# A two-block network on one core: roots applied behind the projections, x in chunks, transposes between pieces

## The chip, the cores and the metric

The kernel runs on one core of a Trainium2 chip, in one launch. The metric is the time of the launch on the device in microseconds. Three runs of the kernel before gave 2681.14, 2683.04 and 2679.93 us, median 2681.14.

## The reference, cut to what matters

Two small networks of two layers each are applied to one sequence of 256 tokens and 2048 features, in float32. The change touches the first network alone:

```python
def first_block(x, ...):                   # x: (1, 256, 2048)
    for layer in range(2):
        h = rmsnorm(x, norm_gains[layer])  # x * rsqrt(mean(x^2) + eps) * gain
        x = x + (even_layer if layer == 0 else odd_layer)(h, ...)
    return rmsnorm(x, final_norm_gain)
```

The even layer projects h to a recurrent branch (x part and gate, a convolution over 4 tokens, two gate matrices, a scan) and to sliding-window attention (q, k, v, gate), and projects the mix back. The odd layer projects h to latents with norms of their own (from which the queries, keys and values of one attention come), to a gate for it, and to a differential attention (q, k, v, gate), and projects back. Since a projection is linear, the root of a token can be multiplied before it (into h) or behind it (into its result).

## The kernel before

**Stages and pieces.** The list `STAGES` (line 52) holds the projections in order: lru, kv, swa, out0 (layer 0), cq, diff, mla, out1 (layer 1), then ret, four, out2, conv, out3 (second network). A stage has units (4 in lru, swa, out0, diff and mla, 3 in cq, 1 in kv), and a unit has 8 pieces, or 16 in diff. A piece is a weight tile of mostly 128x1024 floats (512 KB). All pieces go through a ring of four slots: SP loads `w_raw`, ScalarE rounds it to `w_hi` (line 712), VectorE computes `w_lo` = `w_raw` - `w_hi` (line 1334), and TensorE multiplies w_hi by the high part of the activations, w_hi by the low part, and w_lo by the high part (lines 2010 to 2013 where features are the rows of the result, 2025 to 2028 where tokens are). ScalarE may write a slot when the piece four before is used, SP may load it when w_lo of that piece is done.

**Order.** Each engine walks the pieces in the order of the stages and runs a hook behind each piece p of a unit. In it the epilogue of the unit before is done, step by step (functions `lru`, `swa`, `cq`, `diff`, `mla`, one of each name per engine): the eviction of the projections from PSUM in the hook of piece 2, scores on TensorE in the hook of piece 0 (swa) or 1 (diff, mla), the largest scores, exponentials, transposes and values later. In the last unit of a stage the epilogue lies in the hooks of the next stage; in mla two steps of diff share one hook. The order is written out by hand, and each engine executes strictly in its order. Most pieces let TensorE begin with w_hi alone; the last piece of a unit, and the first in stages with more than two banks (diff among them; mla is exempt), wait for w_lo first (`project`, lines 2057 to 2059).

**Banks.** lru, swa, cq and the out stages have two pairs of banks, used in turn (`PAIRS`, line 64); kv, diff and mla have one set. `enter` (line 2031) is TensorE's wait for the eviction of a bank's contents, counted by `s_free`. In diff the banks are 0 (q), 1 (k), 2 and 3 (v and gate of each tile of 128 tokens); in mla bank 2 takes the gate in pieces 0 to 3, and the others are filled later.

**The ada sums.** For the second network VectorE multiplies 256 KB pieces of a weight by two condition vectors, two operations of 128x512 a step (line 1323). `_units` (line 79) says behind which pieces: in swa 0, 1, 5, 6; in out0 from unit 1 and in cq from unit 1 all; in diff 0 to 4 and 9 to 13; in mla 4 to 7 from unit 1. The step stands behind the hook of its piece.

**The entries of both layers.** `norm` on TensorE (line 2228) transposes x, 32 blocks of 128x128, into the banks 0 to 6 (pairs of features tiles), broadcasts the roots of the tokens with a matmul of ones by a diagonal matrix (line 2251), and transposes the last pair. ScalarE has squared x (line 725 for the first layer; line 755 chunk by chunk for the others), VectorE computes the root with one Newton step (`root`), then multiplies each transposed tile by gain and root (line 1389), ScalarE rounds it (line 718), VectorE takes the difference (line 1399). SP first loads the two tiles of x, then weights; ScalarE's queue loads 15 sets of parameter rows, and GpSimd's queue constants, sinks, decays, lambdas and the gate weights.

Of the kernel before, what the change touches and what calls it, by code (L numbers as in the profile page):

```python
# [28 lines left out]
N_PARAM, N_MISC = (7, 8), 7  # L29
# [34 lines left out]
PAIRS = {"lru": ((0, 1), (2, 3)), "swa": ((2, 3), (0, 1)), "cq": ((0, 1), (2, 3)), "four": ((2, 3), (0, 1)),  # L64
# [98 lines left out]
def build(nc, d, out, stop_after=None):  # L163

    ctx = ExitStack()
    with ctx:
# [43 lines left out]
        acc_c = sb("acc_c", [P, 2, ADA_N])  # L210
        cn = sb("c_norm", [P, CQ_T + CKV_T, 2 * T], F32R)
# [63 lines left out]
        s_par = [sem("first_params_landed"), sem("other_params_landed")]  # L275
        s_ident = sem("identity_landed")
        s_misc = sem("small_inputs_landed")
        s_x = [sem(f"x_landed{t}") for t in range(TT)]
# [25 lines left out]
        s_n = {k: sem(f"norm_{k}") for k in ("sum", "mean", "root", "diag", "rows", "rows_sb", "psum", "tile", "hi", "lo")}  # L304
        s_added = sem("residual_added")
# [9 lines left out]
        for stage, names in {  # L315
            "lru": ("conv", "gates", "gate", "tanh", "sig", "y"),
            "swa": ("gate", "scores", "max", "exp", "prob", "probT", "probT_sb", "o", "y"),
# [48 lines left out]
        NORM_BANKS = {0: 0, 1: 8, 3: 16, 4: 24, 5: 32}  # L366

# [52 lines left out]
        def _(sp):  # L420
            for t in range(TT):
                sp.dma_start(x[:, t, :], d["x"][0, t * P:(t + 1) * P, :]).then_inc(s_x[t], 16)
# [4 lines left out]
            def sources(stage, i, p):  # L427
# [29 lines left out]
                if stage == "cq":  # L457
                    w = d["l1_w_in"].rearrange("(t p) n -> p t n", p=P)
                    n = 320 if isinstance(i, int) and i == 2 else 512
                    return [(lambda r: r[:, 0:2 * n].rearrange("p (t n) -> p t n", t=2),  # L460
                             w[:, 2 * p:2 * p + 2, ds(512 * i, n)])]
# [72 lines left out]
        def view(ap, *dims):  # L534
            names = " ".join("abc"[:len(dims)])
            return ap.rearrange(f"p ({names}) -> p {names}", **dict(zip("abc", dims)))

# [108 lines left out]
        def _(pool):  # L646
            nc.gpsimd.memset(y[:, 0:3 * P], 0.0)
            nc.gpsimd.memset(ones[:, :], 1.0).then_inc(s_set, 1)
            pool.dma_start(const_a[:, :], d["const_a"][:, P:]).then_inc(s_misc, 16)
# [12 lines left out]
            gates(0)  # L662
            with pool.Fori(1, COUNT["lru"]) as i:
# [38 lines left out]
        def _(sc):  # L702
# [17 lines left out]
            def norm_sums(k, src, ready):  # L720

                for t in range(TT):
                    ready(t)
                    nc.scalar.drain()
                    last = nc.scalar.activation(scr_a[:, 0:D] if k == 0 else junk, src[:, t, :], ACT.Square,
                                                accum_out=stat[:, 0, t:t + 1])
                last.then_inc(s_n["sum"], 1)
# [10 lines left out]
            def norm_hi(k, dst, order, bias=None):  # L738

                buffers = norm_scratch(k)[0]  # L740
                for n in order:
                    tmp = halves(buffers[:, n % buffers.shape[1], :])
                    sc.wait_ge(s_n["tile"], NORM_BANKS[k] + n + 1)
                    if bias is None:
                        last = copy(dst[:, 2 * n:2 * n + 2, 0:T], tmp)
                    else:
                        for h in range(2):
                            last = nc.scalar.activation(dst[:, 2 * n + h, 0:T], tmp[:, h, :], ACT.Identity,
                                                        bias=bias(2 * n + h))
# [539 lines left out]
        def _(ve):  # L1289
# [213 lines left out]
            def kv(p, i=0):  # L1503
                pass
# [1103 lines left out]
```

## Time and profile before

| | |
|---|---|
| median of three runs | 2681.14 us (2679.93 to 2683.04) |
| span of the profiled execution | 2678.8 us (first to last instruction) |
| TensorE matmuls | 2612.4 us, 98% |
| VectorE | 1708.0 us, 64% |
| ScalarE | 1280.1 us, 48% |
| GpSimd | 23.0 us, 1% |
| DMA | 536.51 MB, 200 GB/s in the mean |

The profile gives the span of one execution; its whole time lies in what the runs show, 1.1 to 4.2 us above the span. The page gives for each engine its busy time; for the matmuls the ends are modelled, so that overlapping ones are counted once. In the list of waits of an engine each row is a line that waited, the line it waited for, the total in us, how often and the longest. In a timeline a row is start and duration in us, engine, line, operation, result <- operands and the number of merged instructions; a bracket shows the idle time of the engine before it and what released it.

### The profile page before, as it was taken

What the parts mean: (1) busy time and instruction counts of PE and PEld (TensorE: products, weight loads), DVE (VectorE), ACT (ScalarE), POOL (GpSimd) and SP (SyncE); (2) the same over time, 40 slices, a digit from 0 to 9 for tenths busy, and PEclk for the clock granted to TensorE, in tenths of its full rate; (3) what the DMA queues carried; (4) which work ended last, traced back from release to release, by engine and by line L of the source; (5) the groups of instructions that cost most, each with busy time, mean ns of one, the idle gap of its engine ahead of it and who ended that gap; (6) DMA issues with size and microseconds to landing.
All of it is one profiled execution on the core that took longest, in us unless ns stands there. A gap on an engine that the chain in (4) does not pass through costs nothing.

```text
span 2678.8 us, 40094 instructions
## 1 busy us (share of the span) xinstructions
PE 2612.4 (98%) x14747; PEld 2292.4 (86%) x14747; DVE 1708.0 (64%) x2212; ACT 1280.1 (48%) x1795; POOL 23.0 (1%) x42
## 2 busy tenths in 40 slices
PE   7999999999999999999999999999999999999998
PEld 6999878888977899999999988878888888888886
DVE  5768888875786755455556565567875555555644
ACT  4767444555557444344453344444444444444443
POOL 1000000000000000000000000000000000000000
PEclk9999999999999999999999999999999999999999
DMA  6565867874666555555566766657975556566664
GB/s 190 163 208 174 271 196 235 249 233 134 208 222 200 178 179 187 166 180 178 179 196 224 230 199 204 191 173 258 295 255 185 187 188 189 188 190 188 207 192 141
DMA packets 451671, 536.51 MB, mean 200 GB/s; under 512 B 33147, under 2 KB 343958, under 8 KB 450646
## 3 DMA queue, kind: packets, MB, share of 16 engines
q1 hardware_dynamic: 448128, 522.29, 62.0%
q0 software_dynamic: 2720, 12.21, 1.5%
q8 instruction: 85, 1.39, 0.2%
q10 hardware_dynamic: 694, 0.26, 0.0%
q14 instruction: 44, 0.36, 0.0%
HBM read 532.56 MB, written 2.10 MB: 200 GB/s over the span
## 4 chain that ended last, share of the span: by engine, by line
PE 91%; DVE 4%; ACT 2%; issue 1%; DMA 1%; DVEq 1%; ACTq 0%; SPq 0%
PE banks L2025 20%; PE banks L2026 20%; PE banks L2028 20%; PE banks L2010 7%; PE banks L2013 7%; PE banks L2011 7%; DVE w_lo L1334 1%; PE banks L2454 1%; DMA w_raw<-in_l_w_in 1%; PE banks L2212 1%; ACT w_hi L712 1%; PE banks L2509 1%; PE banks L2495 1%; PE banks L2485 1%; PE banks L2475 1%
## 5 line engine op out<-in xcount | busy, mean ns | idle before, releaser
L1334 DVE TENSOR_TENSOR w_lo<-w_raw,w_hi 128x1024 fp32r<-128x1024 f32 (+2 forms) x840 | 975.1, 1168 | 653.1 <-ACT w_hi L712 623.6
L712 ACT ACTIVATE w_hi<-w_raw 128x1024 fp32r<-128x1024 f32 (+2 forms) x840 | 842.9, 1013 | 903.8 <-PE banks L2028 744.4
L2025 PE MATMUL banks<-w_hi,act_hl 128*128 128x512 f32 (+2 forms) x2496 | 961.8, 386 | 8.8 <-DVE scr_a L1389 2.5
L2026 PE MATMUL banks<-w_hi,act_hl 128*128 128x512 f32 (+2 forms) x2496 | 956.5, 384 | 0.0
L2028 PE MATMUL banks<-w_lo,act_hl 128*128 128x512 f32 (+2 forms) x2496 | 693.4, 383 | 0.0
L2025 PEld LDWEIGHTS banks<-w_hi,act_hl 128*128 128x128 f32 x2496 | 471.0, 189 | 99.2 <-issue 3.7
L2026 PEld LDWEIGHTS banks<-w_hi,act_hl 128*128 128x128 f32 x2496 | 471.4, 189 | 83.9 <-issue 0.2
L2028 PEld LDWEIGHTS banks<-w_lo,act_hl 128*128 128x128 f32 x2496 | 457.5, 189 | 83.4
L2010 PE MATMUL banks<-act_hl,w_hi 128*128 128x256 f32 x1696 | 446.8, 293 | 15.1 <-ACT scr_a L718 4.9
L2011 PE MATMUL banks<-act_hl,w_hi 128*128 128x256 f32 x1696 | 431.0, 284 | 0.0
L2010 PEld LDWEIGHTS banks<-act_hl,w_hi 128*128 128x128 f32 x1696 | 325.5, 192 | 28.0 <-issue 14.2
L2011 PEld LDWEIGHTS banks<-act_hl,w_hi 128*128 128x128 f32 x1696 | 326.1, 192 | 4.0 <-issue 0.7
L2013 PE MATMUL banks<-act_hl,w_lo 128*128 128x256 f32 x1696 | 288.6, 285 | 0.0
L2013 PEld LDWEIGHTS banks<-act_hl,w_lo 128*128 128x128 f32 x1696 | 251.1, 192 | 4.8
L718 ACT ACTIVATE scr_b<-banks 128x512 f32<-128x512 f32 (+1 forms) x112 | 56.3, 504 | 93.2 <-PE banks L2478 34.8
L1323 DVE SCALAR_TENSOR_TENSOR acc_x<-y_mix,silu_c,acc_x 128x512 f32<-128x512 f32 x120 | 89.6, 746 | 1.7
L1323 DVE SCALAR_TENSOR_TENSOR acc_x<-const_b,silu_c,acc_x 128x512 f32<-128x512 f32 x120 | 89.5, 746 | 1.5
L1323 DVE SCALAR_TENSOR_TENSOR acc_c<-ada_ring,silu_c,acc_c 128x512 f32<-128x512 f32 x120 | 89.5, 746 | 0.6
L1323 DVE SCALAR_TENSOR_TENSOR acc_x<-ada_ring,silu_c,acc_x 128x512 f32<-128x512 f32 x120 | 89.4, 745 | 0.0
L718 ACT ACTIVATE scr_a<-banks 128x512 f32<-128x512 f32 (+3 forms) x64 | 38.4, 640 | 44.0 <-PE banks L2311 30.6
L850 ACT ACTIVATE scr_a<-scr_a,soft 128x128 f32<-128x128 f32 x80 | 35.3, 442 | 29.1 <-DVE soft L1522 29.1
L1005 ACT ACTIVATE scr_b<-banks 128x256 f32<-128x256 f32 x16 | 6.0, 382 | 78.5 <-PE banks L2454 78.5
(301 smaller groups left out, 1589.7 us busy)
## 6 DMA issues: line engine op xcount, KB each, us to landing
w_raw<-in_od_w_in SPq DMA_DIRECT2D x256, 512.0 KB, 4.0
w_raw<-in_ev_w_in SPq DMA_DIRECT2D x256, 256.0 KB, 3.6
w_raw<-in_l_w_in SPq DMA_DIRECT2D x96, 512.0 KB, 4.4
w_raw<-in_l_w_in SPq DMA_DIRECT2D x128, 256.0 KB, 3.5
ada_ring<-in_ada_w SPq DMA_DIRECT2D x128, 256.0 KB, 4.2
w_raw<-in_l_w_out SPq DMA_DIRECT2D x64, 512.0 KB, 4.7
y_mix<-in_ada_w SPq DMA_DIRECT2D x128, 256.0 KB, 3.1
const_b<-in_ada_w SPq DMA_DIRECT2D x128, 256.0 KB, 4.7
```

The costliest lines, as they stand in the source:

```text
L712: last = nc.scalar.activation(dst(w_hi[:, p % RING, :]), src(w_raw[:, p % RING, :]), ACT.Copy)
L718: return nc.scalar.activation(dst, src, ACT.Copy, **k)
L850: last = nc.scalar.activation(v[:, h, lo:hi], v[:, h, lo:hi], ACT.Exp, bias=soft[:, 1, 2 * h + b:2 * h + b + 1], accum_out=soft[:, 2, 2 * ...
L1323: last = stt(acc, w, cond, acc, ALU.mult, ALU.add)
L1334: last = tt(dst(w_lo[:, p % RING, :]), src(w_raw[:, p % RING, :]), dst(w_hi[:, p % RING, :]).bitcast(F32), ALU.subtract)
L2010: mm(out, hi, a[:, kt, 0:T], start=start, stop=False, skip_group_check=True)
L2011: r = mm(out, hi, a[:, kt, T:2 * T], start=False, stop=False, skip_group_check=True)
L2013: r = mm(out, lo, a[:, kt, 0:T], start=False, stop=stop, skip_group_check=True)
L2025: mm(out, ah, hi, start=start, stop=False, skip_group_check=True)
L2026: r = mm(out, al, hi, start=False, stop=False, skip_group_check=True)
L2028: r = mm(out, ah, lo, start=False, stop=stop, skip_group_check=True)
L2212: last = mm(PS[:, bank, at:at + 1], acc[:, b * P:(b + 1) * P], ones[:, 0:1], start=True, stop=True, skip_group_check=True)
```

## The change

1. SP loads x in four chunks of 512 features (both token tiles), each ahead of one of the first weight pieces, and takes over most parameter rows, behind pieces 3, 4 and 5. ScalarE's queue loads the identity and the gains alone. GpSimd waits for two used pieces before its loads, and loads the constants last.
2. In the first network x is transposed without the root: ScalarE rounds gain times x from PSUM, VectorE computes the difference from PSUM. The pairs of tiles are transposed between the pieces of the first unit of lru, and, for the second layer, between pieces of the last unit of out0 and the first of cq, in another order of the features (`TURN_ORDER`), with the weights of cq in that order.
3. The root is computed meanwhile and broadcast to `root_row`. Where the result has tokens in the free dimension (lru, kv's keys, q and gate of swa, q and k of diff, gate of mla), VectorE evicts it, times `root_row` (`leave`, `mla_gate`); where tokens are the partitions (values of kv, cq, v and gate of diff), ScalarE evicts it with the root as scale.
4. cq's pairs of banks are exchanged, and TensorE's waits are fitted.

```diff
-PAIRS = {..., "cq": ((0, 1), (2, 3)), ...
+PAIRS = {..., "cq": ((2, 3), (0, 1)), ...
 def _(sp):
-            for t in range(TT):
-                sp.dma_start(x[:, t, :], d["x"][0, t * P:(t + 1) * P, :]).then_inc(s_x[t], 16)
+            x_chunk(0)
...
                         for dst, src in pieces:
                             sp.dma_start(dst(w_raw[:, p % RING, :]), src).then_inc(s_w[p % RING], 16)
+                        if stage == "lru" and first == 0 and p < 3:
+                            x_chunk(p + 1)
+                        if stage == "lru" and first == 0 and 3 <= p < 6:
+                            parameter_rows(p - 3)
...
 def _(pool):
-            pool.dma_start(const_a[:, :], d["const_a"][:, P:]).then_inc(s_misc, 16)
+            pool.wait_ge(s_used, 2)
...
             gates(0)
+            pool.dma_start(const_a[:, :], d["const_a"][:, P:]).then_inc(s_misc, 16)
...
 def _(sc):
+            def turned_high(k, n):
+                pair, b = TURN_ORDER[k][n], turned_bank(k, n)
+                sc.wait_ge(s_n["psum"], NORM_BANKS[k] + n + 1)
...
+                for h in range(2):
+                    last = copy(act[:, 2 * pair + h, 0:T], half_of(b, h), scale=pcol(gains, 2 * pair + h))
+                last.then_inc(s_n["hi"], 1)
 def lru
-                if p == 2:
+                if p == 3:
                     sc.wait_ge(s["y"], i + 1)
-                    full(sc, "lru", i, 1)
-                    copy(lru_x[:, :, 3:259], halves(pair_bank("lru", i, 0))).then_inc(s_free, 1)
-                    full(sc, "lru", i, 2)
-                    copy(lru_g, pair_bank("lru", i, 1)).then_inc(s_free, 1)
+                    sc.wait_ge(s_free, bank_count("lru", i, 2))
 def diff
                     sc.wait_ge(s["y"], i + 1)
-                    full(sc, "diff", i, 1)
-                    copy(at_q, bank(A), scale=64 ** -0.5).then_inc(s_free, 1)
-                    full(sc, "diff", i, 2)
-                    copy(at_k, bank(B)).then_inc(s_free, 1)
+                    sc.wait_ge(s_free, bank_count("diff", i, 2))
                     full(sc, "diff", i, 3)
-                    copy(at_v[:, 0:T], half_of(C, 0))
+                    copy(at_v[:, 0:T], half_of(C, 0), scale=stat[:, 3, 0:1])
...
+            split("lru")(0, placed({
+                0: highs(0, 0, 1), 1: highs(0, 2), 2: highs(0, 3), 3: highs(0, 4),
+                4: [*highs(0, 5), lambda: input_square(0)],
+                5: [*highs(0, 6), lambda: input_square(1).then_inc(s_n["sum"], 1)],
+                6: [*highs(0, 7), lambda: norm_root(0)]}))
...
 def _(ve):
+            def turned_low(k, n):
+                ve.wait_ge(s_n["hi"], NORM_BANKS[k] + n + 1)
+                for h in range(2):
+                    f = 2 * pair + h
+                    last = stt(act[:, f, T:2 * T], half_of(b, h), pcol(gains, f), act[:, f, 0:T].bitcast(F32),
+                               ALU.mult, ALU.subtract)
...
+            def leave(stage, i, n, dst, scale=None):
+                full(ve, stage, i, n)
+                src = halves(pair_bank(stage, i, n - 1) if stage in PAIRS else bank(BANKS[stage][n - 1]))
+                if scale is None:
+                    r = tt(dst, src, root_by_token(), ALU.mult)
+                else:
+                    r = stt(dst, src, scale, root_by_token(), ALU.mult, ALU.mult)
+                r.then_inc(s_free, 1)
 def lru
                 if p == 2:
-                    ve.wait_ge(s_free, bank_count("lru", i, 1))
+                    drain()
+                    leave("lru", i, 1, lru_x[:, :, 3:259])
+                    leave("lru", i, 2, halves(lru_g))
+                    drain()
 def swa
+                if p == 2:
+                    drain()
+                    leave("swa", i, 1, halves(swa_q), SWA_D ** -0.5)
+                    leave("swa", i, 2, halves(swa_g))
 def diff
+                if p == 2:
+                    drain()
+                    leave("diff", i, 1, halves(at_q), 64 ** -0.5)
+                    leave("diff", i, 2, halves(at_k))
...
+            def mla_gate(i):          # called in the hook of piece 7 of unit i
+                drain()
+                ve.wait_ge(s_used, pieces_before("mla", i) + 4)
+                tt(halves(at_g), halves(bank(C)), root_by_token(), ALU.mult).then_inc(s_free, 1)
...
+            split("lru")(0, placed({
+                0: lows_of(0, 0, 1), 1: lows_of(0, 2), 2: lows_of(0, 3), 3: lows_of(0, 4), 4: lows_of(0, 5),
+                5: lows_of(0, 6), 6: [*lows_of(0, 7), lambda: block_root(0)],
+                7: [first_parameters, lambda_sums, clear_history]}))
...
 def _(te):
+                if stage == "diff" and isinstance(i, int) and i == 0:
+                    v = bank_count("cq", 1, 2) if n < 3 else bank_count("cq", 2, n - 2)
...
+            gain_columns()
+            turn(0, 0)
+            turn(0, 1)
+            stage_loop(te, "lru", run("lru"), lru_and_columns, placed({
+                **{p: turns(0, p + 2) for p in range(5)}, 5: [*turns(0, 7), first_columns], 6: [lambda: root_rows(0)]}))
...
+                def turns_in_out0(p, i):
+                    if i == COUNT["out0"] - 2 and 1 <= p < 7:
+                        turn(1, p - 1)
...
-                norm(1, x, first_columns, lambda: te.wait_ge(s_free, BANK0["cq"]))
-                run("cq")(0, nothing, 0)
+                run("cq")(0, placed({1: turns(1, 6), 2: turns(1, 7), 6: [lambda: root_rows(1)]}), 0)
```

## Rows read from the trace of the kernel before

**Rows 1.** The page, part 1: busy time, share and instructions of each engine.
```profile
PE 2612.4 (98%) x14747; PEld 2292.4 (86%) x14747; DVE 1708.0 (64%) x2212; ACT 1280.1 (48%) x1795; POOL 23.0 (1%) x42
```
**Rows 2.** Waits of TensorE over the span: total us, times, longest.
```profile
PE banks L2010 <- ACT scr_a L718: 4.9, 4, 2.1
...
PE banks L2025 <- ACT scr_a L928: 0.8, 2, 0.4
```
**Rows 3.** Timeline of the start and of the second unit of lru.
```profile
18.27 1.06 ACT L712 ACTIVATE w_hi<-w_raw 128x1024 fp32r<-128x1024 f32 x1 [2.73 <-DMA w_raw<-in_l_w_in]
22.82 0.58 PE L2010 MATMUL banks<-act_hl,w_hi 128*128 128x256 f32 x1 [3.63 <-DVE act_hl L1399]
48.24 0.55 PE L2010 MATMUL banks<-act_hl,w_hi 128*128 128x256 f32 x1 [2.85 <-DVE w_lo L1334]
54.81 1.12 PE L2013 MATMUL banks<-act_hl,w_lo 128*128 128x256 f32 x8
57.69 1.12 PE L2013 MATMUL banks<-act_hl,w_lo 128*128 128x256 f32 x8
```
**Rows 4.** Line 422, the two loads of x: from issue to landing.
```profile
DMA to landing us min/median/max: 5.2/7.2/9.2
```
**Rows 5.** Timeline: a square of x, two tile products, an output product.
```profile
10.00 1.91 ACT L725 ACTIVATE scr_a<-x_res 128x2048 f32<-128x2048 f32 x1
24.94 0.87 DVE L1389 SCALAR_TENSOR_TENSOR scr_a<-banks,param_cols,scr_a 128x256 f32<-128x256 f32 x2
199.24 0.69 DVE L1555 TENSOR_TENSOR y_mix<-banks,scr_a 128x512 f32<-128x512 f32 x1 [3.82 <-PE banks L2319]
```
**Rows 6.** Stretches: length, busy times (count), granted clock, DMA share, GB/s.
```profile
22.82:27.82 5.00, 5.00 (x23) 5.00 (x24) 3.77 (x6) 2.52 (x3) 0.00 (x0) 0.51 0.47 150
48.24:52.68 4.44, 4.43 (x24) 4.44 (x25) 3.37 (x3) 3.53 (x5) 0.00 (x0) 0.62 0.61 174
629.00:640.00 11.00, 8.89 (x63) 8.32 (x63) 4.83 (x5) 5.22 (x7) 0.00 (x0) 0.84 0.52 172
420.00:430.00 10.00, 8.29 (x58) 7.93 (x57) 9.63 (x15) 5.86 (x12) 0.00 (x0) 1.00 0.97 317
```
**Rows 7.** Timeline of out0 to cq and of cq to diff.
```profile
344.96 1.22 DVE L1334 TENSOR_TENSOR w_lo<-w_raw,w_hi 128x1024 fp32r<-128x1024 f32 x1
354.85 3.22 PE L2238 MATMUL banks<-ident,x_res 128*128 128x128 f32 x28
364.08 0.80 PE L2025 MATMUL banks<-w_hi,act_hl 128*128 128x512 f32 x1 [2.49 <-DVE scr_a L1389]
427.78 0.36 PE L2010 MATMUL banks<-act_hl,w_hi 128*128 128x256 f32 x1 [1.71 <-DVE w_lo L1334]
```
**Rows 8.** Timeline in unit 2 of swa: scores, and w_lo of pieces 2, 3.
```profile
205.07 1.68 PE L2304 MATMUL banks<-scr_a 64*128 64x128 f32 x16
206.26 2.36 DVE L1334 TENSOR_TENSOR w_lo<-w_raw,w_hi 128x1024 fp32r<-128x1024 f32 x2
```
**Rows 9.** Timeline where units 1 and 2 of diff begin.
```profile
475.74 1.23 DVE L1334 TENSOR_TENSOR w_lo<-w_raw,w_hi 128x1024 fp32r<-128x1024 f32 x1
477.43 0.50 PE L2025 MATMUL banks<-w_hi,act_hl 128*128 128x512 f32 x1
527.21 0.28 PE L2010 MATMUL banks<-act_hl,w_hi 128*128 128x256 f32 x1
528.72 1.23 DVE L1334 TENSOR_TENSOR w_lo<-w_raw,w_hi 128x1024 fp32r<-128x1024 f32 x1
527.49 1.28 ACT L928 ACT_TABLE_LOAD   x1
528.78 0.39 ACT L928 ACTIVATE scr_a<-banks 128x256 f32<-128x256 f32 x1
529.22 0.50 PE L2025 MATMUL banks<-w_hi,act_hl 128*128 128x512 f32 x1 [0.41 <-ACT scr_a L928]
```
**Rows 10.** Timeline at the end of mla: scores of the last unit.
```profile
762.23 1.66 PE L2411 MATMUL banks<-k_rope,scr_a 64*128 64x128 f32 x8 [4.58 <-DVE scr_a L1636]
```

More of the change, by code:

```diff
@@ L718, in copy, with input_square @@
                 return nc.scalar.activation(dst, src, ACT.Copy, **k)
[L720 to L727, printed above, removed]
+            def input_square(t):
+                if t == 0:
+                    for c in range(4):
+                        sc.wait_ge(s_x[c], 16)
+                nc.scalar.drain()
+                return nc.scalar.activation(scr_a[:, 0:D], x[:, t, :], ACT.Square, accum_out=stat[:, 0, t:t + 1])
+            def turned_high(k, n):
+                pair, b = TURN_ORDER[k][n], turned_bank(k, n)
+                gains = G_L0 if k == 0 else G_L1
+                sc.wait_ge(s_n["psum"], NORM_BANKS[k] + n + 1)
+                if k == 0 and n == 0:
+                    sc.wait_ge(s_pc, 1)
+                if k == 1:
+                    sc.wait_ge(s_used, pieces_before("out0", 3) + pair + 1 if pair >= 4 else pieces_before("out0", 0))
+                for h in range(2):
+                    last = copy(act[:, 2 * pair + h, 0:T], half_of(b, h), scale=pcol(gains, 2 * pair + h))
+                last.then_inc(s_n["hi"], 1)
             def root_table():
@@ L742, in norm_hi @@
                     tmp = halves(buffers[:, n % buffers.shape[1], :])
[L743 to L749, printed above, removed]
+                    sc.wait_ge(s_n["tile"], NORM_TILES[k] + n + 1)
+                    for h in range(2):
+                        last = nc.scalar.activation(dst[:, 2 * n + h, 0:T], tmp[:, h, :], ACT.Identity,
+                                                    bias=bias(2 * n + h))
                     last.then_inc(s_n["hi"], 1)
@@ L959, in mla @@
                     full(sc, "mla", i, 5)
-                    copy(at_g, bank(C)).then_inc(s_free, 1)
+                    sc.wait_ge(s_free, bank_count("mla", i, 1))
                     copy(mla_qr0, PS[:, 4, 0:T], scale=MLA_SCALE).then_inc(s_free, 1)
@@ L1503, in kv @@
             def kv(p, i=0):
-                pass
+                if p == 2:
+                    full(ve, "kv", 0, 2)
+                    for g in range(2):
+                        last = tt(kT4[:, 2 * g:2 * g + 2, :], halves(bank(A))[:, g:g + 1, :].broadcast_to([P, 2, T]),
+                                  root_by_token(), ALU.mult)
+                    last.then_inc(s_free, 1)
             def scores_max(s_tile, heads, mask, first_bank, done, sink=None):
@@ L2253, in norm, with turn @@
                 r.then_inc(s_n["rows"], 1)
[L2254 to L2255 removed]
+            def turn(k, n):
+                pair, b = TURN_ORDER[k][n], turned_bank(k, n)
+                if k == 0:
+                    te.wait_ge(s_x[n // 2], 16)
+                else:
+                    te.wait_ge(s_free, bank_count("out0", 3 - pair // 2, 2))
+                buffers = 4 if k == 0 else 3
+                if n >= buffers:
+                    te.wait_ge(s_n["lo"], NORM_BANKS[k] + n - buffers + 1)
+                for h in range(2):
+                    f = 2 * pair + h
+                    for t in range(TT):
+                        c = h * T + t * P
+                        r = nc.tensor.transpose(PS[:, b, c:c + P], x[:, t, f * P:(f + 1) * P], ident[:, :])
+                r.then_inc(s_n["psum"], 1)
             def context_pair(b):
```

244 lines of the change are left out of this document (138 added, 106 removed).

## Prediction

> **What bounds the kernel now.** I read the page first: TensorE is busy for 2612.4 of the 2678.8 us [rows 1], so only what stops TensorE, or slows its clock, can be gained or lost. The waits of TensorE come next [rows 2]: evictions that hold it up are there already (4.9 us before line 2010, 0.8 us before line 2025). Then the timelines. At the start TensorE stands until 22.82, and again for 2.85 us before 48.24 [rows 3]. Between pieces it repeats one pattern: the low products start at 54.81 and again at 57.69, so a piece costs 2.88 us at full clock [rows 3]. Everything else that counts is how far VectorE and ScalarE are ahead of TensorE where one unit follows another, since both walk the pieces in order and do a unit's epilogue in the hook of the next unit's piece 2.
>
> The clock. In the stretch behind a 3.63 us stop it is granted at 0.51, behind 2.85 us at 0.62, behind 2.11 us at 0.84 over 11 us, and behind 1.71 us (420 to 430) at 1.00 [rows 6]; 0.5 is 1.2 GHz, 1.00 is 2.4 GHz. So a stop of over 2 us costs (1 - 0.51) x 5.0 = 2.5, (1 - 0.62) x 4.44 = 1.7 or (1 - 0.84) x 11 = 1.8 us more, and one of 1.7 us nothing. I take 1.8 for a long stop and half of it for one of 1.9 to 2.0 us, which lies between. The Trainium skill (TensorE: Matmul & The Clock Gate, Part 1) says that the place where the clock changes shifts from run to run; by that the half stops could come out either way in different runs.
>
> **Part 1, the start (a gain).** The first piece waited for all of x (2 MB, landing after 5.2 and 9.2 us, 7.2 in the middle [rows 4]), its sums, the root, and for the weights, which landed only at 18.27 behind x and everything else [rows 3]. Now 512 KB of x and then piece 0 stand first in SP's queue, the parameter rows follow piece 3, and GpSimd's broadcasts and constants wait for two used pieces. Half of a tile that took 5.2 us should be there at 4 to 5 us, the weights at 6 to 7: I take 6.4. Then w_hi 1.06 [rows 3], w_lo 1.23 [rows 9], two lows 0.87 [rows 5], each behind the other on VectorE: 6.4 + 3.2 = 9.6 for the first product, against 22.82; bounds 8.5 and 12. From there to the end of the ninth piece: 9 x 2.88 = 25.9; a cold first piece 2.2 (as before, part of the 2.5); 24 transposes at 3.22/28 = 0.115 us [rows 7], 2.8; the row sums of the roots and a parameter transpose 0.6. Then the stops that stay: ScalarE's two squares of 1.91 us and a read each [rows 5] stand ahead of w_hi of pieces 5 and 6 (about 0.5 each), and the root chain on VectorE stands ahead of w_lo of piece 7, which the last piece of a unit wants whole (2.4). Sum 9.6 + 25.9 + 2.2 + 2.8 + 0.6 + 3.4 = 44.5; before it was 54.81 + 0.96 = 55.8 [rows 3]. Gain 11.3. Behind it the parameter arithmetic on VectorE (some 4 us), two evictions more and the copied root row no longer lie under that slack: I give back 1.8 in units 1 and 2, and 0.8 for half a clock fall at piece 7. Net gain 8.7 (bounds 5 and 12).
>
> **Part 2, out0 to cq (a gain).** Before, out0's last product ends where the first of 28 transposes starts, at 354.85; the root and the rest follow, and cq starts at 364.08 [rows 7], with a piece of 12 products at the low clock (2.5 us by rows 6). Now latent transposes stand between pieces, with the scales applied behind. 364.08 - 354.85 = 9.2, plus 2.5, less 32 transposes (3.7) and the root rows (0.5): 7.5. VectorE does two lows more (1.7 us) in out0's last unit, in which it is otherwise full; it had w_lo of the last piece done at 346.2 [rows 7] and TensorE took it at 352.1, so they are covered. Bounds 5 and 8.5.
>
> **Part 3, cq to diff (a gain).** The 1.71 us before 427.78 [rows 7] end with ScalarE's eviction of cq's last unit: diff's first bank was the same one. With the bank pairs of cq exchanged, diff's banks 0 and 1 are free: 1.7. Bounds 0.5 (VectorE carries the root copy in cq) and 1.7.
>
> **Part 4, mla's gate (a small gain).** The gate's bank is full after piece 3 and was copied only after piece 7. Copied by VectorE in the same unit's piece 7, it is free before the next unit: of the four waits of 4.9 us in [rows 2] the longest, 2.1, is diff to mla, and the other three, 2.8 together, go. Behind the last unit TensorE waits 4.58 us for VectorE's rope [rows 10], and the copy (0.69 [rows 5]) stands ahead of that: -0.75. Net gain 2.0.
>
> **Part 5, the evictions moved to VectorE (a loss).** The root must be multiplied along the free dimension, so q and k of diff, q and gate of swa and both of lru now leave PSUM on VectorE, in the hook of piece 2, that is behind w_lo of piece 2. ScalarE was ahead there; VectorE isn't, since it has two steps of the ada sums (2 x 0.75 us each) between w_lo of pieces 0, 1 and 2. One leave is a tensor-tensor of 128x512 out of PSUM, 0.69 us [rows 5].
>
> swa: scores stand behind piece 0 of the next unit and want q. In unit 2 they started at 205.07, while w_lo of pieces 2 and 3 ran from 206.26 (2.36 for both) [rows 8]: piece 2 is done at 207.48, q leaves at 208.2, so TensorE stops 3.15 us and loses 1.8 of clock: 4.9. The pattern repeats twice, less late: in unit 3 without a mix in between (scores at 233.11, w_lo from 233.16, q out at 235.1: 2.0) and in out0, where scores come at once (258.28; w_lo of piece 2 ends at 259.43, q out at 260.15: 1.9). Both 1.9 to 2.0: another 2 x 0.9. Sum 10.6. The first unit is free of it (VectorE has no output to wait for).
>
> diff: one set of banks, so piece 0 of the next unit itself wants bank 0. In unit 2 TensorE was there at 527.21 [rows 9]; w_lo of piece 2 starts at 528.72 and ends at 529.95, q is out at 530.7, k at 531.3: a stop of 3.5 us. Now ScalarE, which waits for k, does v (as long as the silu), loads a table (1.28) and does the first silu (0.39) [rows 9] before bank 2 is free: 533.4, while it was entered at 529.22. That is 4.2 us, and 0.4 for what is left of the low clock. Unit 3 repeats it (w_lo of piece 2 from 578.75): 4.7. At unit 1 VectorE is less late (w_lo of piece 2 from 475.74 [rows 9], TensorE ready at 475.81): bank 0 at 477.7, bank 2 at 480.45 against 477.43 [rows 9], so 3.0 + 0.3. At diff to mla ScalarE's chain moves by 0.4. Sum 13.0. Bounds: nothing, if something keeps VectorE ahead that I don't see; 16, with each clock fall full.
>
> lru: two leaves more (1.4 us) before the convolution, whose result is wanted only behind piece 2, where it had over 3 us: free. VectorE's kT4 and ScalarE's scaled v4 in kv: free, for swa's first banks are others.
>
> For one step a page speaks against what I took: the Trainium skill (ScalarE: Activation LUTs, What ACT_TABLE_LOAD costs) puts a table switch at 1.28 us and 1.38 us of drain. The row shows the silu 0.01 us behind the load [rows 9]: no drain. By the page each of four joins would be 1.4 us worse, 5.5 us in all; nothing here rests on it.
>
> **Sum.** -8.7 - 7.5 - 1.7 - 2.0 + 10.6 + 13.0 = +3.7 us. The profile's span is 2678.8 and the runs, with what lies around it, 2679.93 to 2683.04, median 2681.14, so 2.3 us around; the forecast is 2678.8 + 3.7 + 2.3 = 2684.8. The change moves some 20 us out of two joins and the start and puts 24 us into six others.
>
> **The rivals.** (a) Faster: VectorE's lateness costs half or less. It would take stops that overlap with others or a VectorE that comes earlier to piece 2; for it speaks that its ada steps wait for nothing, so any slack comes back to it. The place is the hook of piece 2 in swa and diff, and it decides when part 5 is below 14 us: at half, 2681.1 + 3.7 - 11.8 = 2673. With part 5 at nothing it is 2661. Against it: before each of these joins VectorE waits for something that answers to TensorE (the output of the unit before, or ScalarE's w_hi that waits for a used piece), so its distance to TensorE is fixed. (b) Clearly slower: the start brings little. VectorE waits in piece 7 of the first unit for seven small inputs, among them 0.7 MB of constants, which GpSimd now issues at 19 us or later; TensorE wants w_lo of the next piece at about 44. If they land after 42, or the first weights at 9 us, the start gives 4 instead of 8.7, and every clock fall comes full: 2684.8 + 4.7 + 3 = 2692. (c) The join of out0 and cq turns into a new stop, since ScalarE waits there for transposes before w_hi of the next pieces: 2 to 4 us, 2688.
>
> **Chances.** The forecast (gains and stalls as summed, within 3 us) 0.55; (a) 0.17; (b) 0.13; (c) 0.15. No change within 0.2% means 2675.8 to 2686.5, which is about what a measurement of this kernel can tell. Of the forecast's 0.55 about 0.4 lies in it, of (a) 0.03, of (c) 0.04; faster 0.14 from (a); the rest, 0.39, is slower. Range for 8 in 10: 2673 to 2692, from (a) at half cost to (b).
>
> **What would show it.** The first product at 9 to 10 us, the ninth piece done near 45. No stop between out0 and cq. New stops of TensorE before the scores of swa (3.1, 2.0, 1.9 us) whose releaser is VectorE's new eviction line, and before piece 0 of diff's units 1 to 3 (2, 3.5, 3.5 us), each followed by a wait for ScalarE's silu. The prediction is wrong if those stops are below 1 us, if the first product comes after 12 us, or if mla's three waits stay.

## The result, and the profile after

The changed kernel took 2687.61 us (median of 9 runs, 2685.54 to 2690.48) against 2681.14 us of the kernel before (9 runs, 2678.03 to 2684.06). The ratio is 1.0027, with a 95% interval of 1.0019 to 1.0036: slower, by a little more than can be told from no change. The forecast was 2684.8 us. The profiled execution took 2687.05 us over a span of 2685.4, so 1.65 us lie around the span, where the prediction had taken 2.3.

The page says only that TensorE is still nearly always busy [rows 1]; its busy time is 3.9 us longer, for nearly the same number of products (below, the same 16 products take 3.09 us at the low clock and 1.69 at the full one):

```profile
PE 2616.3 (97%) x14748; PEld 2294.3 (85%) x14748; DVE 1716.8 (64%) x2227; ACT 1270.1 (47%) x1783; POOL 23.1 (1%) x42
```

The waits of TensorE (total, times, longest) name what is new. L1471 is VectorE's new eviction `leave` with a scale; L1719 is the rope, L764 a copy of ScalarE:

```profile
PE banks L2103 <- DVE scr_a L1471: 8.9, 3, 3.5
PE banks L2415 <- DVE scr_a L1471: 7.5, 3, 3.5
PE banks L2523 <- DVE scr_a L1719: 5.7, 1, 5.7
...
PE banks L2103 <- ACT scr_a L764: 3.0, 1, 3.0
PE banks L2103 <- DVE act_hl L1448: 2.3, 1, 2.3
```

16.4 us of waits end with the eviction, for the scores of three units of swa (the last of them lies in out0) and for three units of diff. In the timeline of the start, the first product is at 10.11 where it was at 22.82 [rows 3], behind w_hi, w_lo and two low conversions, one behind the other; the last row is the later stop for w_lo of piece 7:

```profile
5.87 1.97 PE L2367 MATMUL banks<-ident,x_res 128*128 128x128 f32 x8
6.96 1.06 ACT L758 ACTIVATE w_hi<-w_raw 128x1024 fp32r<-128x1024 f32 x1 [3.62 <-DMA w_raw<-in_l_w_in]
8.05 1.22 DVE L1372 TENSOR_TENSOR w_lo<-w_raw,w_hi 128x1024 fp32r<-128x1024 f32 x1 [1.88 <-ACT w_hi L758]
9.19 1.65 DVE L1448 SCALAR_TENSOR_TENSOR act_hl<-banks,param_cols,act_hl 128x256 fp32r<-128x256 f32 x4
10.11 0.58 PE L2103 MATMUL banks<-act_hl,w_hi 128*128 128x256 f32 x1 [2.28 <-DVE act_hl L1448]
38.37 0.36 PE L2103 MATMUL banks<-act_hl,w_hi 128*128 128x256 f32 x1 [0.51 <-DVE w_lo L1372]
```

Where out0 becomes cq, the transposes lie between pieces and no bracket with idle time stands anywhere near; before there was a block from 354.85 to 364.08 [rows 7]:

```profile
357.22 0.60 PE L2367 MATMUL banks<-ident,x_res 128*128 128x128 f32 x4
357.58 0.48 PE L2118 MATMUL banks<-w_hi,act_hl 128*128 128x512 f32 x1
360.43 0.39 PE L2118 MATMUL banks<-w_hi,act_hl 128*128 128x512 f32 x1
```

The joins in swa (timeline, unit 2, and the stops of the other two). VectorE finishes w_lo of piece 2 at 198.4, has a gap of 0.45 us for which the profile names no cause, and evicts q until 199.55; TensorE stands for 3.54 us in all, and the 16 score products take 3.09 us where they took 1.68 [rows 8], at the low clock:

```profile
197.19 1.23 DVE L1372 TENSOR_TENSOR w_lo<-w_raw,w_hi 128x1024 fp32r<-128x1024 f32 x1
198.86 0.69 DVE L1471 SCALAR_TENSOR_TENSOR scr_a<-banks,root_row 128x512 f32<-128x512 f32 x1 [0.45 <-issue]
199.61 3.09 PE L2415 MATMUL banks<-scr_a 64*128 64x128 f32 x16 [3.54 <-DVE scr_a L1471]
232.25 3.01 PE L2415 MATMUL banks<-scr_a 64*128 64x128 f32 x16 [2.05 <-DVE scr_a L1471]
260.98 1.69 PE L2415 MATMUL banks<-scr_a 64*128 64x128 f32 x16 [1.92 <-DVE scr_a L1471]
```

In diff, unit 2. VectorE ends an ada step, does w_lo, then the two evictions; ScalarE waits 5.64 us for the second and only then copies v, loads a table and does the silu, for which TensorE stops again:

```profile
525.52 0.75 DVE L1361 SCALAR_TENSOR_TENSOR acc_x<-ada_ring,silu_c,acc_x 128x512 f32<-128x512 f32 x1
526.36 1.23 DVE L1372 TENSOR_TENSOR w_lo<-w_raw,w_hi 128x1024 fp32r<-128x1024 f32 x1
527.69 0.69 DVE L1471 SCALAR_TENSOR_TENSOR scr_a<-banks,root_row 128x512 f32<-128x512 f32 x1
528.29 0.68 DVE L1469 TENSOR_TENSOR scr_a<-banks,root_row 128x512 f32<-128x512 f32 x1
528.52 0.36 PE L2103 MATMUL banks<-act_hl,w_hi 128*128 128x256 f32 x1 [3.51 <-DVE scr_a L1471]
529.06 0.47 ACT L764 ACTIVATE scr_a<-banks,stat 128x256 f32<-128x256 f32 x1 [5.64 <-DVE scr_a L1469]
529.54 1.28 ACT L972 ACT_TABLE_LOAD   x1
530.83 0.47 ACT L972 ACTIVATE scr_a<-banks,stat 128x256 f32<-128x256 f32 x1
531.36 0.80 PE L2118 MATMUL banks<-w_hi,act_hl 128*128 128x512 f32 x1 [0.59 <-ACT scr_a L972]
```

The other two joins stop 1.92 us and then 1.17 us (472.20, 475.03), and 3.52 us (585.20); diff to mla stops 3.02 us (642.23). The clock behind these stops, in stretches (length, busy time of TensorE and number of its products, granted clock, DMA share, GB/s):

```profile
200.00:206.00 6.00, 6.00 (x35) 0.58 0.62 206
232.00:238.00 6.00, 5.75 (x37) 0.72 0.71 215
260.00:266.00 6.00, 5.03 (x31) 1.00 0.64 233
472.00:478.00 6.00, 4.63 (x29) 1.00 0.71 243
528.00:534.00 6.00, 4.88 (x18) 0.61 0.69 238
534.00:540.00 6.00, 6.00 (x38) 0.82 0.64 171
585.00:591.00 6.00, 5.80 (x20) 0.52 0.32 96
```

In these rows 1.00 is 2.4 GHz; a value between 0.5 and 1.00 is a mean over a stretch that has both levels. The same work on TensorE in both timelines gives the account:

| work | before | after | after - before |
|---|---|---|---|
| ninth piece done | 55.93 | 44.36 | -11.6 |
| first scores of swa | 177.03 | 167.96 | -9.1 |
| probabilities transposed, swa unit 2 | 218.29 | 215.31 | -3.0 |
| the same, unit 3 | 246.34 | 247.04 | +0.7 |
| the same, last unit, in out0 | 268.66 | 271.44 | +2.8 |
| ada sum in cq | 415.34 | 410.65 | -4.7 |
| latents transposed in diff | 444.79 | 439.10 | -5.7 |
| probabilities transposed, diff unit 1 | 503.28 | 500.93 | -2.4 |
| unit 2 | 555.10 | 559.39 | +4.3 |
| unit 3 | 605.02 | 615.14 | +10.1 |
| the last, in mla | 649.49 | 660.41 | +10.9 |
| first product of ret | 873.34 | 879.93 | +6.6 |
| span | 2678.8 | 2685.4 | +6.6 |

### The profile page after: what moved, and what is told of

It is laid out like the page before. It is cut to its first block, busy times and chain, and to the rows that moved or that the text cites. A ratio compares the mean times of both kernels' runs of the same rounds, so it can differ in the third digit from the quotient of the medians.

```text
span 2685.4 us, 40126 instructions
## 1 busy us (share of the span) xinstructions
PE 2616.3 (97%) x14748; PEld 2294.3 (85%) x14748; DVE 1716.8 (64%) x2227; ACT 1270.1 (47%) x1783; POOL 23.1 (1%) x42
## 4 chain that ended last, share of the span: by engine, by line
PE 89%; DVE 5%; ACT 2%; DVEq 2%; issue 1%; DMA 0%; ACTq 0%; SPq 0%
PE banks L2118 20%; PE banks L2119 20%; PE banks L2121 20%; PE banks L2103 7%; PE banks L2104 7%; PE banks L2106 7%; DVE w_lo L1372 2%; PE banks L2566 1%; DVEq L1363 1%; PE banks L2307 1%; PE banks L2415 1%; DVE acc_x L1361 1%; ACT w_hi L758 1%; PE banks L2621 1%; PE banks L2597 1%
## 5 line engine op out<-in xcount | busy, mean ns | idle before, releaser
L764 ACT ACTIVATE scr_b<-banks 128x512 f32<-128x512 f32 (+1 forms) x112 | 56.2, 503 | 94.4 <-PE banks L2590 35.1
```

The costliest lines, as they stand in the source:

```text
L764: return nc.scalar.activation(dst, src, ACT.Copy, **k)
```

## The experiments

Each was timed in five rounds beside the kernel before on the same chip, but not all on one chip; so what is compared between kernels is the ratio to it. That of the changed kernel is 1.0027. Of the span, the part from the first product of ret to the end is the same program in all of these kernels, and it took 1805.3 to 1807.9 us: 2 us of any single trace are of that kind.

**The ada steps moved away from the joins (e1, and e2 in diff only).**

```diff
-_units = [("swa", i, (0, 1, 5, 6)) ...
-... ("diff", i, (0, 1, 2, 3, 4, 9, 10, 11, 12, 13)) ...
+_units = [("swa", i, (5, 5, 6, 6)) ...           # e1 alone
+... ("diff", i, (2, 3, 4, 5, 7, 9, 10, 11, 12, 13)) ...
```

> The changed kernel, with the two steps of the ada sums that stand behind pieces 0 and 1 of each unit moved: in swa to pieces 5 and 6 (0, 1, 5, 6 becomes 5, 5, 6, 6), in diff to 5 and 7. Nothing else. Theory A (VectorE reaches the evictions behind w_lo of piece 2 about 3.0 us too late because of these two steps of 1.5 us): the six new stops of TensorE go (swa 3.5, 2.05, 1.9 us; diff 1.9, 3.5, 3.5), with the low clock behind them. That is 11.9 us in swa and 16.6 us in diff, so about 2687.6 - 28 + 1 = 2660 us (2656 to 2665). Theory B (the eviction on VectorE is late in any case, since it stands behind w_lo of piece 2 and two evictions follow each other): stops of 1 to 2 us stay, 2672 to 2676 us. Theory C (VectorE has no room elsewhere in swa, which it fills for 25 of 28 us): the stops move to the last piece of swa's units, 2668 us or more, with TensorE waiting for w_lo.

2673.14 us, ratio 0.9973 (0.9961 to 0.9984): 14.5 us below the changed kernel and faster than the kernel before, but half of what theory A gave, and inside the range of theory B. By the trace swa (first scores to last transposes) took 96.0 us against 103.5 in the changed kernel, so 7.5 of the 11.9 us went, and diff 10.0 of the 16.6. The timeline says where the rest is:

```profile
197.35 1.68 PE L2415 MATMUL banks<-scr_a 64*128 64x128 f32 x16 [0.17 <-DVE scr_a L1471]
220.44 0.39 PE L2103 MATMUL banks<-act_hl,w_hi 128*128 128x256 f32 x1 [0.90 <-DVE w_lo L1372]
253.54 1.70 PE L2415 MATMUL banks<-scr_a 64*128 64x128 f32 x16 [1.92 <-DVE scr_a L1471]
518.34 0.36 PE L2103 MATMUL banks<-act_hl,w_hi 128*128 128x256 f32 x1 [0.80 <-DVE scr_a L1471]
521.17 0.50 PE L2118 MATMUL banks<-w_hi,act_hl 128*128 128x512 f32 x1 [1.17 <-ACT scr_a L972]
626.04 0.36 PE L2103 MATMUL banks<-act_hl,w_hi 128*128 128x256 f32 x1 [3.03 <-ACT scr_a L764]
```

swa's first stop went from 3.54 to 0.17, as A has it. The third, 1.92, stayed: out0's first unit has no ada steps, so there was nothing to take away there, which I had overlooked; behind it the clock fell (0.72 from 253.5 to 259.5). In diff each join keeps about 0.8 and 1.17 (5.8 us in all): the eviction still stands behind w_lo of piece 2, and ScalarE's chain behind the eviction. That is theory B's share. The stop at diff to mla, 3.03 us, is as long as in the changed kernel: it waits for ScalarE's copy. A little of C is there too (0.90 before 220.44, for w_lo).

> Only the steps of diff moved (behind pieces 2, 3, 4, 5, 7 instead of 0 to 4). Theory A: diff's stops go, 16.6 us, swa's stay: 2671 us (2668 to 2674), 11 to 12 us above the kernel with both moved. Theory B: 2678 or more. If the clock behind diff's stops were only worth the 1.8 us each that the prediction took, the gain would be 13 instead: 2674.6.

2680.43 us, ratio 0.9997 (0.9989 to 1.0006): 8.0 us less than the changed kernel by the ratios, where theory A wanted 16.6. In its trace diff, from its first wait for bank 2 to mla's first piece, took 209.3 us against 219.1 in the changed kernel: 9.8 of the 16.6. What is left is for the most part 5.9 us of stops of e1's kind, 0.7 to 0.9 and 1.17 us at each join.

**Half the dose (e4).** swa (1, 5, 5, 6), diff (1, 2, 3, 4, 5, 9, ...).

> Half of the dose: one of the two steps in front of piece 2 moved, in swa 1, 5, 5, 6, in diff 1, 2, 3, 4, 5, 9 to 13. Theory A: VectorE is 1.5 us earlier, so the stops shrink to 2.0, 0.5, 0.4 us in swa and 0.4, 2.0, 2.0 us in diff; those of 2.0 still bring some low clock (1.7 us each as behind the 2.05 us stop), so 7 us less in swa and 7 in diff: 2673.5 us (2670 to 2677). If the clock falls only behind stops longer than these, another 3 to 5 us go: 2669. Theory B: hardly any change, 2684 or more.

2677.12 us, ratio 0.9988 (0.9979 to 0.9996), 10.5 us less, at the upper edge of theory A's range. One step of 1.5 us fewer shortened the stops in swa to 1.68, 0.55 and 1.92, those in diff to 0.84, 2.37 and 2.01: by 1.1 to 1.9 us each, except the one in out0. So the length of these stops follows VectorE's place: 1.5 us of work taken away in front of the eviction shortens the stop by about as much.

**The evictions on ScalarE again (e3).** q and gate of swa, q and k of diff with a constant scale. The kernel leaves out the root of the token in these four, so it computes something else; it is there for its time alone.

```diff
-                    leave("diff", i, 1, halves(at_q), 64 ** -0.5)      # VectorE
-                    leave("diff", i, 2, halves(at_k))
...
+                    copy(at_q, bank(A), scale=64 ** -0.5).then_inc(s_free, 1)   # ScalarE
+                    copy(at_k, bank(B)).then_inc(s_free, 1)
```

> The ada steps stay where they are; q and gate of swa, q and k of diff leave PSUM on ScalarE again, plain copies with a constant scale. It leaves out the root of the token in these four, so the output is another. Theory A (only the place of the eviction in VectorE's order costs): about the same as with the ada steps moved, 2660 us (2656 to 2666), no stop of TensorE before the scores of swa nor before piece 0 of diff. Theory D (the new stops come from something else of the change, such as the broadcast root, the later weights or the changed positions of DMAs): the stops stay, 2680 us or more.

2663.36 us, ratio 0.9936 (0.9923 to 0.9948), 24 us less with the ada steps untouched, inside theory A's range. No stop of TensorE at a join of swa or diff ends with an eviction of VectorE any more; the largest left of the joins are these:

```profile
PE banks L2103 <- ACT scr_a L764: 2.5, 1, 2.5
...
PE banks L2415 <- ACT scr_a L764: 1.2, 1, 1.2
```

With e1 and e4, which leave the eviction on VectorE and change only what stands ahead of it, that shows the cause of part 5: the engine that evicts, and where in its order. The edit of e3 touches nothing else of the change. It also gives the worth of the rest: all gains without part 5 are some 17 us against the kernel before, where the prediction's terms had 19.9.

**The eviction one piece earlier (e10).** The hook of piece 1 on VectorE; ScalarE copies v and does the silu before it waits; mla's first entry waits for bank 2 alone.

```diff
-                if p == 2:
+                if p == 1:
                     drain()
                     leave("diff", i, 1, halves(at_q), 64 ** -0.5)
...
-                    sc.wait_ge(s_free, bank_count("diff", i, 2))
                     full(sc, "diff", i, 3)
...
+                    sc.wait_ge(s_free, bank_count("diff", i, 2))
+                    nc.scalar.drain().then_inc(s_free, 1)
```

> Only the place of the evictions: hook of piece 1 instead of 2 on VectorE in swa and diff, ScalarE's v and first silu ahead of its wait, mla's first entry waits for bank 2 alone; the ada steps stay where they are. VectorE is 2.7 us less late (one w_lo of 1.23 and one ada step of 1.5 us lie behind the eviction now). Theory A: stops of 3.5, 3.5, 3.5 us shrink to about 0.8 each and those of 1.9 to 2.05 to nothing, with the clock full: swa -11, diff -14, diff to mla -3.5: 2659 to 2663 us. Theory B (VectorE has too much to do around a join; what is not late in the eviction is late in w_lo of piece 2): 2668 or more, with TensorE waiting for w_lo.

2665.6 us, ratio 0.9939 (0.9926 to 0.9952), 22 us less by the medians, with the ada steps where they were. That is 3 us above theory A's range; two of the five runs took 2661 and three 2665.6. The stops for bank 0 in diff are now 0.87 and 0.88 us, as expected, and none at the first join. Not as expected, three of 0.6 to 0.9 us are left in swa's epilogue (before the scores at 251.88 and the transposes at 210.98 and 262.94), and 1.82 us at diff to mla. The first row is the join of units 1 and 2 of diff, the second is diff to mla:

```profile
514.71 0.36 PE L2104 MATMUL banks<-act_hl,w_hi 128*128 128x256 f32 x1 [0.87 <-DVE scr_a L1472]
618.29 0.36 PE L2104 MATMUL banks<-act_hl,w_hi 128*128 128x256 f32 x1 [1.82 <-ACTq L973]
```

**Control (e8).** The kernel before with e1's ada steps.

> Control: the kernel before, with only the ada steps moved as in the first experiment (swa 5, 5, 6, 6; diff 2, 3, 4, 5, 7, 9 to 13). Theory A (VectorE's order matters only because the change put evictions into it): no stop of TensorE in swa or diff of the kernel before ended with VectorE's work of a join, so nothing but the 0.4 us stops moves: 2680 to 2681.5 us. Rival (the moved steps are an improvement by themselves, and the gain of 14 us over the changed kernel says little about the evictions): 2676 or less.

2680.06 us, ratio 0.9997 (0.9988 to 1.0006), as theory A has it: nothing that can be told. Moving the steps is worth something only where VectorE has an eviction to be late for.

**The start: x whole first (e5), GpSimd at once (e6), parameter rows early (e6b).**

```diff
-            x_chunk(0)
+            for c in range(4): x_chunk(c)          # e5
...
-                            x_chunk(p + 1)         # e5
...
-            pool.wait_ge(s_used, 2)                # e6
...
-                        if ... and 3 <= p < 6:
-                            parameter_rows(p - 3)
+                        if ... and p < 3:          # e6b
+                            parameter_rows(p)
```

> The changed kernel with the four chunks of x all issued ahead of the first weight piece, instead of one ahead of each of the first four pieces; nothing else. Theory S (the start gains because the first piece of weights need only wait for a quarter of x): the first piece of weights now lands behind 2 MB of x, 1.5 MB later; at the 356 GB/s that the DMAs moved in this stretch of the changed kernel that is 4.2 us, so the first product starts at 13 to 14.5 us instead of 10.1, and the ninth piece ends 2 to 4 us later, since the stops behind it are those of ScalarE's squares and the root: 2689.5 to 2691.5 us. Rival R (what brought the start forward is that the parameter rows and GpSimd's constants no longer stand in the way, or that the root is no longer waited for; the order of x does not matter): below 1 us, 2687 to 2688.5.

2690.46 us, ratio 1.0038 (1.0025 to 1.0051), 2.9 us more. The intervals overlap, but the trace agrees: the first product came at 14.28, 4.2 us later, and the first product of ret 2.8 us later:

```profile
14.28 0.58 PE L2102 MATMUL banks<-act_hl,w_hi 128*128 128x256 f32 x1 [6.54 <-DVE act_hl L1447]
```

> The changed kernel without GpSimd's wait for two used pieces: its small loads, the gate weights and 0.7 MB of constants are issued at once, beside x and the first weights. Theory S (early traffic is what holds the first pieces up): the constants and gates share the DMAs with the first 2 MB of x and weights, the first product starts 1 to 3 us later than at 10.1, and half or all of that stays: 2688.5 to 2690.5 us. Rival R (the wait brings nothing, since the chain of ScalarE's and VectorE's conversions sets the first product): 2687 to 2688. By the rival of the prediction, that the late constants hold VectorE up in piece 7, the kernel would get faster, by the 0.7 us stop that is left there: 2686.9.

2687.76 us, ratio 1.0026 (1.0015 to 1.0036): rival R, no difference that can be told. The trace shows small effects: the first product at 10.75, and a stop of 1.48 us at the third piece for its weights. The stop for the root was the same 0.96 and 0.51 us, so the late constants of the prediction's rival (b) were not late.

```profile
17.18 0.36 PE L2102 MATMUL banks<-act_hl,w_hi 128*128 128x256 f32 x1 [1.48 <-ACT w_hi L757]
```

> The changed kernel with the parameter rows (14 small loads in three groups) behind the weight pieces 0, 1 and 2 instead of 3, 4 and 5, so ahead of the chunks of x for the next pieces no more than a few small loads. Theory S: each load takes SP some time to issue, so the second to fourth chunk and piece come 0.5 to 1 us later, but they were not late (no stop of TensorE between 10.1 and 29.3): no difference, 2687 to 2688.5 us. Rival: these rows were what delayed the weights before, and the first stop grows: 2690 or more.

2686.38 us, ratio 1.0019 (1.0010 to 1.0028): 0.6 us below theory S's range, but no difference that can be told. Of the three edits of the start that were tried, the chunks are worth 3 us and the other two less than can be told. Their first products came 4.2, 0.6 and 0.2 us later, and 12.7 us are between the kernel before and the changed one: most of the rest should be the root and the whole of x that the first product no longer waits for, but no experiment shows it.

**out0 to cq: no transposes in out0 (e7).**

```diff
-                    if i == COUNT["out0"] - 2 and 1 <= p < 7:
-                        turn(1, p - 1)
+                turn(1, 0)
+                turn(1, 1)                         # behind out0's last product
```

> The transposes for the second layer, six pairs of which stood between the pieces of the last unit of out0, begin only when out0's last product is done: two pairs ahead of cq's first piece, two behind its first and second piece each, one behind the third and fourth; ScalarE and VectorE convert the first two ahead of cq's first weights. The root stays behind the projections. Theory I (the 7.5 us between out0 and cq come from the transposes and their conversions lying beside products): TensorE stops again at cq's first piece for the transposes' conversions (0.8 + 0.9 us) and for w_hi and w_lo behind them (1.06 + 1.23), some 3 to 4 us, with 2.5 us of low clock behind it: 2692.5 to 2695 us. Rival W (the gain comes from the root not being waited for, which this kernel keeps): below 1.5 us, 2687.5 to 2689.

2694.89 us, ratio 1.0045 (1.0033 to 1.0057): 7.3 us more by the medians and 4.8 by the ratios, since one of the six runs took 2686.24 and the other five 2692.5 to 2695.5. That is theory I. Behind out0 stand two stops, 2.21 us and, seven us later, 1.52 for w_hi; the clock behind the first was granted at 0.72 (361.5 to 367.5):

```profile
361.50 0.47 PE L2118 MATMUL banks<-w_hi,act_hl 128*128 128x512 f32 x1 [2.21 <-DVE act_hl L1448]
```

In the trace diff's first wait for bank 2 came 6.6 us later than in the changed kernel, of which 0.6 lay there before this join. So most of the 7.5 us at this join is the interleaving.

**A better version (e9, e12).** e10 with the ada steps moved (swa 3, 5, 5, 6; diff as in e1), and the last rope of mla in the hook of piece 0 of out1; e12 adds one line to ScalarE in diff:

```diff
+                    nc.scalar.activation(junk[:, 0:1], ones[:, 0:1], ACT.Silu)
                     full(sc, "diff", i, 3)
```

> A version that takes what the first four kernels showed: ada steps moved (swa 3, 5, 5, 6; diff 2, 3, 4, 5, 7, 9 to 13), VectorE's evictions in the hook of piece 1 instead of 2 (ahead of w_lo of piece 2), ScalarE copies v and does the first silu of diff before it waits for VectorE's evictions, mla's first entry waits for bank 2 alone, and the last rope of mla comes behind piece 0 of out1 instead of 2. Theory A (each stop is the length of a chain that starts with VectorE's place in its order): diff's stops (0.65 + 1.2, 0.8 + 1.2, 0.8 + 1.2 with the ada steps moved) and swa's 1.9 and 0.9 go, -8.5; the 3.0 at diff to mla shrinks to about 0.5 with its clock, -4; the rope's 5.7 to 2.5 to 3, -3 to -6: 2673.1 - 16 to -18, so 2655 to 2658. Theory B (the evictions wait for the end of the projections anyway, and VectorE then holds up w_lo of piece 2): stops of 1 us remain in each unit before w_lo, 2663 or more.

2659.48 us, ratio 0.9923 (0.9910 to 0.9936), 1.5 us above theory A's range. The rope's stop fell from 5.55 in e10 to 0.75 us, but new ones of 1.01 and 2.69 us stand behind it (the probabilities, and the mix that VectorE now does later): from the products of mla's last rope (734.03, 735.43 in e10) to ret the two kernels differ by 1.6 us only.

> The improved version, and ScalarE loads the table of the silu ahead of its wait for the projections in diff (a silu of one column), so that the load of 1.28 us is not between the copy of v and the silu. Theory A (the 1.8 us stop at diff to mla and the three of 0.3 us in diff are the copy, the table load and the silu in a row): the stops shrink to about 0.5 and 0: 2659.5 - 1.3 - 0.9 = 2657.3 us (2656 to 2658.5). Rival: another wait is as late (the end of the projections of the last bank, or VectorE's eviction), so less than 0.7 us: 2659 or more.

2656.03 us, ratio 0.9908 (0.9892 to 0.9923): 25 us or 0.9% faster than the kernel before, 1.2% faster than the changed one, and 3.5 us less than e9 by the medians. By the stops that shrank the table is worth 2.4 of these: 1.5 at diff to mla and 0.3 at each of three joins in diff, whose stops are gone. Another 1.3 us lie ahead of the edit: the last scores of swa stand at 249.87 in this trace and at 251.13 in e9's. The stop at diff to mla is 0.35 us instead of 1.82, because the load of the table ends before bank 2 is full (ScalarE's timeline):

```profile
608.45 1.28 ACT L969 ACT_TABLE_LOAD   x1
610.79 0.47 ACT L764 ACTIVATE scr_a<-banks,stat 128x256 f32<-128x256 f32 x1 [0.84 <-PE banks L2123]
611.79 0.35 PE L2105 MATMUL banks<-act_hl,w_hi 128*128 128x256 f32 x1 [0.35 <-ACTq L974]
```

## Why the prediction was right

The time lay inside the range, and the sign of the sum and of each of its six terms was right. By its own steps (forecast, then measured from the account above):

- **Part 1**, -8.7: -9.1. The first product came at 10.1 where 9.6 was worked out, the ninth piece ended at 44.36 where 44.5 was worked out. In part that is luck, since the terms of that sum missed both ways: the stops of the first unit were 0.74, 0.96 and 0.51 us, 2.2 in all, where 3.4 were taken, and the first product came 0.5 later. In the kernel before the ninth piece ended at 55.93, not 55.8, as its last row takes 1.12 us and not 0.96. 2.5 us were given back, most of them in the next unit, 2.6 forecast; its stops were 0.69, 0.18 and 0.39 us, and the clock stayed at 1.00.
- **Part 2**, -7.5: -7.5 (+2.8 to -4.7). No stop was left. e7 shows the mechanism.
- **Part 3**, -1.7: -1.0. The 1.71 us are gone. Their row in the kernel before names VectorE's w_lo, not the eviction that the prediction names; both ended within 0.1 us of each other there, and in e8 the same stop, 1.15 us, is put to ScalarE's copy, so the reading holds. In the changed kernel diff's banks 2 and 3 are entered 0.3 us and some tenths late instead, for cq's last eviction on ScalarE.
- **Part 5, swa**, +10.6: +11.9. The stops were 3.54, 2.05 and 1.92 us, forecast 3.15, 2.0 and 1.9.
- **Part 5, diff**, +13.0: +16.6. The stops of bank 0 were 1.92, 3.51 and 3.52, forecast 2, 3.5 and 3.5. This is the mis-sized term: not the stops but the clock behind them. I had charged 0.3 to 0.4 us at each join, since I took the second wait to end whatever the low clock had cost. Measured, (1 - 0.61) x 6 + (1 - 0.82) x 6 = 3.4 us behind the second and (1 - 0.52) x 6 = 2.9 behind the third. The wait for the silu was only 0.59 us behind the second, where it hid little, and the third had none, against the prediction's sign of a wait for the silu behind each. At diff to mla the stop grew by 0.9, forecast 0.4.
- **Part 4**, -2.0: -4.3. mla's three waits went, worth 3.5 us by the times of its units where 2.8 were forecast, and its end came 0.8 later, as forecast. The other 1.6 is luck: in the kernel before the clock was at 0.72 behind a stop of 0.43 us (649.49), and in the changed kernel the same work ran at 1.00 behind a stop of 0.42:

```profile
651.00:657.00 6.00, 6.00 (x40) 0.72 0.64 173
```

So diff cost 3.6 us more than forecast and mla gave 2.3 more, which for the greater part cancel; with 1.3 of swa, 0.7 of part 3 and 0.4 of part 1 the other way the sum is +6.6 where it was +3.7. Parts 3 and 4 have no experiment of their own: their sizes are read from the two timelines alone. Rival (a), lateness at half its cost, is refuted by the stops themselves, which have their full length; with part 5 at nothing the prediction had 2661 us, and e3, which comes near to that, took 2663.36. Rival (b) had a late start, which didn't come; rival (c) a new stop at cq, of which there is none. The table load had no drain in this kernel either: the silu starts 0.01 us behind its end (529.54 + 1.28, 530.83), and the load 0.01 us behind the copy ahead of it, against the 1.38 us of the Trainium skill (ScalarE: Activation LUTs, What ACT_TABLE_LOAD costs); four joins at that price would have been 5.5 us more.

## What to carry to other kernels

When an operation moves from one engine to another, its price is the place that it gets in the new engine's order, not its duration: two evictions of 0.69 us at each of six joins became 28 us in the account (24 of them went in e3), because two ada steps, 3 us, and a w_lo that nobody waited for yet stood ahead of them, and because another engine's chain stood behind them. Before such a move, list for each join what stands ahead of the operation on the new engine since the last thing it had to wait for, and move either that work (14 us here) or the operation itself, ahead of the conversion that is not yet needed (22 us here, with the other engine's chain shortened). Then look at what the other engine does behind it: work that doesn't depend on the wait, a table load above all, goes ahead of it.

## What the runs showed of the hardware

The low clock does not answer to a stop in a fixed way. A stop of 1.92 us before the last scores of swa left the clock at 1.00 in the changed kernel (260 to 266) and at 0.72 in e1 (253.5 to 259.5). In e4 a stop of 3.03 us was followed by a stretch at 1.00, and the fall came 17 us later, behind a stop of 0.43 us (646.08):

```profile
629.30:635.30 6.00, 6.00 (x51) 1.00 0.47 130
646.00:652.00 6.00, 5.92 (x38) 0.72 0.40 93
```

In the kernel before and in e7 the clock fell in both places, behind the stop at diff to mla and again behind the one of 0.43 us. From mla's first product to the last transposes of diff it took 29.1 to 29.3 us in the changed kernel, e1 and e4, where the clock fell once, and 30.8 us in the kernel before and e7, where it fell twice. The Trainium skill (TensorE: Matmul & The Clock Gate, Part 1) says that the place where the clock changes shifts from run to run; the rows with equal stops and different clocks agree with that. Why a stop of 0.43 us is followed by a fall in some executions and not in others stays open. For a sum it means that each long stop costs 0 to 3.4 us of clock here, and that a difference of 2 us between two traces needs its place named before it is believed.
